# The last mixer's weights split early and kept in DRAM, with four side steps a chunk in its heads

## The reference, cut to what matters

```
x = first_block(x, ...)        # layer 0: short_conv_mixer, layer_norm, conv_ffn, layer_norm
                               # layer 1: diff_attention,   layer_norm, conv_ffn, layer_norm
return second_block(x, ...)    # h += ab_layer(rmsnorm(h)); h += cd_layer(rmsnorm(h)); rmsnorm(h)

def cd_layer(h, w_in, ..., w_glu, b_glu, lower_bound, hgrn_norm_g, w_out):      # the last mixer
    z = h @ w_in
    u, qd, fd, idd, gate = jnp.split(z, CD_SPLIT, axis=-1)
    yc = s5_mixer(u, ...)                      # y = scan over 256 steps; y * sigmoid(y @ w_glu + b_glu)
    f = lower_bound + (1.0 - lower_bound) * jax.nn.sigmoid(fd)
    od = chunked_gated_linear_attention(silu(qd), 1.0 - f, idd, log(f))         # 8 HGRN heads
    y = jnp.concatenate([yc, head_rmsnorm(od, hgrn_norm_g)], -1) * silu(gate)
    return y @ w_out
```

## Time and profile before

| | |
|---|---|
| median of three runs | 3274.36 us |
| profiled execution, its own time | 3276.79 us |
| its span, first to last instruction | 3275.4 us, mean granted TensorE clock 0.974 |
| TensorE matmul busy | 3078.6 us, 94% |
| VectorE busy | 2151.1 us, 66% |
| ScalarE busy | 1526.5 us, 47% |
| DMA | 596.74 MB, mean 182 GB/s |

### The profile page before, as it was taken

The page is one execution under the profiler, slowest core; times in us unless marked ns, Lnnn a source line. Parts: engine busy times, 40 slices in busy tenths (PEclk is TensorE's granted clock), DMA queues, the critical chain, the costliest instruction groups (busy, mean ns, idle before and its releaser), DMA issues. The chain is left out here.

```text
span 3275.4 us, 57220 instructions
## 1 busy us (share of the span) xinstructions
PE 3078.6 (94%) x25870; PEld 2610.3 (80%) x25870; DVE 2151.1 (66%) x2189; ACT 1526.5 (47%) x1393; POOL 65.8 (2%) x112
## 2 busy tenths in 40 slices
PE   8999899999999899998999999997999999788786
PEld 7888688888888787577888888886686787657685
DVE  5555666666555666457687786455665547998785
ACT  4343454545433444745455555334454534424543
POOL 0000000000000000001200000000000001000000
PEclk9999899999999999998999999999999999899898
DMA  8665355555665455453766666652445445554331
GB/s 282 206 206 201 108 206 206 199 200 198 214 206 194 142 176 171 154 168 126 265 227 216 221 225 231 207 193 94 166 155 184 164 168 186 173 196 145 120 121 65
DMA packets 295475, 596.74 MB, mean 182 GB/s; under 512 B 11824, under 2 KB 16048, under 8 KB 295104
## 3 DMA queue, kind: packets, MB, share of 16 engines
q1 hardware_dynamic: 287616, 564.22, 50.4%
q0 software_dynamic: 7616, 28.87, 2.4%
HBM read 577.32 MB, written 15.73 MB: 181 GB/s over the span
## 5 line engine op out<-in xcount | busy, mean ns | idle before, releaser
L1415 DVE TENSOR_TENSOR WL<-WF,WH 128x2048 bf16<-128x2048 f32 x533 | 1206.7, 2285 | 718.9 <-ACT WH L935 718.6
L504 PE MATMUL PSG<-XH,WH 128*128 128x256 bf16 x5648 | 1553.1, 275 | 53.9 <-DVE XL L1484 28.9
L504 PE MATMUL PSG<-XL,WH 128*128 128x256 bf16 x5648 | 1552.7, 275 | 0.0
L504 PE MATMUL PSG<-XH,WL 128*128 128x256 bf16 x5648 | 1552.1, 275 | 0.0
L935 ACT ACTIVATE WH<-WF 128x2048 bf16<-128x2048 f32 x533 | 1000.7, 1899 | 648.8 <-PE PSG L504 416.6
L504 PE MATMUL PSG<-SCR,WH 128*128 128x256 bf16 x4480 | 746.2, 275 | 0.0
L504 PEld LDWEIGHTS PSG<-XH,WH 128*128 128x128 bf16 x5648 | 557.2, 99 | 137.1 <-issue 65.6
L504 PE MATMUL PSG<-SCR,WL 128*128 128x256 bf16 x2240 | 614.8, 274 | 0.0
L504 PEld LDWEIGHTS PSG<-XL,WH 128*128 128x128 bf16 x5648 | 556.9, 99 | 70.5 <-issue 0.6
L504 PEld LDWEIGHTS PSG<-XH,WL 128*128 128x128 bf16 x5648 | 557.2, 99 | 69.2
L504 PEld LDWEIGHTS PSG<-SCR,WH 128*128 128x128 bf16 x4480 | 442.1, 99 | 58.8 <-issue 1.4
(11 more groups left out here) (232 smaller groups left out, 1569.4 us busy)
## 6 DMA issues: line engine op xcount, KB each, us to landing
WF<-ffn_w_up SPq DMA_DIRECT2D x176, 1024.0 KB, 5.8
WF<-ffn_w_down SPq DMA_DIRECT2D x88, 1024.0 KB, 5.1
WF<-ab_w_in SPq DMA_DIRECT2D x56, 1024.0 KB, 5.1
WF<-a_w_in SPq DMA_DIRECT2D x48, 1024.0 KB, 6.4
WF<-cd_w_in SPq DMA_DIRECT2D x48, 1024.0 KB, 5.2
WF<-a_w_out SPq DMA_DIRECT2D x16, 1024.0 KB, 5.2
WF<-kv_w_k SPq DMA_DIRECT2D x16, 1024.0 KB, 5.1
WF<-b_w_q SPq DMA_DIRECT2D x16, 1024.0 KB, 5.1
```

The costliest lines, as they stand in the source:

```text
L504: return nc.tensor.matmul(o, lhsT, rhs, start=start, stop=stop, skip_group_check=True)
L1415: tt(l, w, h, ALU.subtract).then_inc(s_lo, 1)
```

## The change

The kernel makes a plan of positions (`ring_plan`). All 533 chunks are multiplied as before. The 68 chunks of the last mixer are marked "kept": each is also given an earlier position of kind "keep", at which it is loaded in float32, split by ScalarE and VectorE into the next slot of the ring, and not multiplied; SyncE stores the slot's two halves (1 MB) to a DRAM tensor. The keep positions stand behind every fourth chunk of the first mixer's input weights from the ninth on, of up0 and of down0, behind every eighth of up1 and every third of down1. High and low halves now lie side by side in one buffer WS, so that one DMA moves both. At a chunk's own position in the last mixer SyncE loads the halves from DRAM into the slot, once the chunk or the store five positions before is done; ScalarE and VectorE do nothing for it, and TensorE waits on that DMA (d_ws). LA counts ring positions now, keep positions included.

The second change is in the last mixer's rates: four steps a chunk and not three for the second and third gate, glu, the fourth gate and cd_out0, on all three engines.

```
+def ring_plan(groups, stage, count):
+    def span(name):
+        a, b = stage[name][0], stage[name][-1]
+        return groups[a]["first"], groups[b]["first"] + len(groups[b]["rows"])
+    first_kept = span("u")[0]
+    after = set(range(8, span("mix")[1], 4))
+    for name, step in (("up0", 4), ("down0", 4), ("up1", 8), ("down1", 3)):
+        a, b = span(name)
+        after |= set(range(a + 1, b - 1, step))
+    after = sorted(after)[:count - first_kept]
+    plan = []
+    for i in range(count):
+        plan.append(("kept" if i >= first_kept else "mul", i))
+        if i in after:
+            plan.append(("keep", after.index(i)))
+    return plan, first_kept
...
-        WH = sb("WH", [128, RB, 4, 512], BF16)
-        WL = sb("WL", [128, RB, 4, 512], BF16)
+        WS = sb("WS", [128, RB, 2, 4, 512], BF16)
+        WH, WL = WS[:, :, 0, :, :], WS[:, :, 1, :, :]
...
+        def released(p):
+            kind, n = plan[p]
+            return (d_kept[n % 2], 16 * (n // 2 + 1)) if kind == "keep" else (s_mm, n + 1)
+        def split_done(p):
+            if plan[p][0] == "kept":
+                return d_ws[p % RB], 16 * len([q for q in range(p % RB, p + 1, RB) if plan[q][0] == "kept"])
+            return s_lo, raw_number[p] + 1
...
-            def load(i):
-                g, k0, rows = chunks[i]
+            def load(p):
+                if plan[p][0] == "kept":
+                    k = plan[p][1] - first_kept
+                    nc.sync.wait_ge(d_kept[k % 2], 16 * (k // 2 + 1))
+                    nc.sync.wait_ge(*released(p - RB))
+                    nc.sync.dma_start(WS[:, p % RB].rearrange("p h t n -> p (h t n)"), KEPT[k]).then_inc(
+                        d_ws[p % RB], 16)
+                    return
+                i = raw_number[p]
+                g, k0, rows = chunk_at(p)
...
                 if i >= RF:
                     nc.sync.wait_ge(s_lo, i - RF + 1)
                 nc.sync.dma_start(shaped(WF, i % RF, rows, g["width"]), src).then_inc(d_w[i % RF], 16)
+                if i >= RF and plan[raw[i - RF]][0] == "keep":
+                    q = raw[i - RF]
+                    k = plan[q][1]
+                    nc.sync.dma_start(KEPT[k], WS[:, q % RB].rearrange("p h t n -> p (h t n)")).then_inc(
+                        d_kept[k % 2], 16)
...
-                    nc.tensor.wait_ge(s_lo, i + 1)
+                    nc.tensor.wait_ge(*split_done(place[i]))
...
-            for gi in stage["cd_gate"][0:3]:
-                gemm(gi, xh, xl, rate=3)
+            for n, gi in enumerate(stage["cd_gate"][0:3]):
+                gemm(gi, xh, xl, rate=4 if n else 3)
...
-            residual("cd_out0", None, uh, ul, [(s_gl, 5 + k // 4) for k in range(8)], rate=3,
+            residual("cd_out0", None, uh, ul, [(s_gl, 5 + k // 4) for k in range(8)], rate=4,
...
-                if i >= RB:
-                    nc.scalar.wait_ge(s_mm, i - RB + 1)
-                act(shaped(WH, i % RB, rows, g["width"]), shaped(WF, i % RF, rows, g["width"]),
+                if p >= RB:
+                    nc.scalar.wait_ge(*released(p - RB))
+                act(shaped(WH, p % RB, rows, g["width"]), shaped(WF, i % RF, rows, g["width"]),
...
-            def hi_to(i):
-                while state["hi"] <= min(i, len(chunks) - 1):
+            def hi_to(p):
+                while state["hi"] < len(raw) and raw[state["hi"]] <= p:
...
-                    hi_to(g["first"] + c + LA)
+                    hi_to(place[g["first"] + c] + LA)
```

More of the change, by code:

```diff
@@ L227, in two_block_model @@
         d_w = [sem(f"d_w{i}") for i in range(RF)]
+        d_kept = [sem(f"d_kept{i}") for i in range(2)]
+        d_ws = [sem(f"d_ws{i}") for i in range(RB)]
         d_out = [sem(f"d_out{i}") for i in range(2)]
@@ L266, in two_block_model, with chunk_at @@
         groups, stage, chunks = weight_groups(A)
+        plan, first_kept = ring_plan(groups, stage, len(chunks))
+        KEPT = nc.dram_tensor("kept_weights", (len(chunks) - first_kept, 128, 2 * 2048), BF16).ap()
+        place = {n: p for p, (kind, n) in enumerate(plan) if kind != "keep"}
+        raw = [p for p, (kind, _) in enumerate(plan) if kind != "kept"]
+        raw_number = {p: n for n, p in enumerate(raw)}
+        def chunk_at(p):
+            kind, n = plan[p]
+            return chunks[n + first_kept if kind == "keep" else n]
+        def released(p):
+            kind, n = plan[p]
+            return (d_kept[n % 2], 16 * (n // 2 + 1)) if kind == "keep" else (s_mm, n + 1)
[3 more added lines that the diff above has]
+            return s_lo, raw_number[p] + 1
         def evac(gi):
@@ L422, in sync_program @@
             nc.sync.dma_start(POSI, A["positions"].partition_broadcast(128)).then_inc(d_pos, 16)
-            for i in range(RF, len(chunks)):
-                load(i)
+            for p in range(RF, len(plan)):
+                load(p)
             for g in range(4):
@@ L1372, in scalar_program @@
             for j, gi in zip(GATE_ORDER[0:3], gates[0:3]):
[L1373 removed]
+                keep(gi, four(GT1, j), 4 if j != 2 else 3, func=ACT.Silu)
             side.until(s5_flow)
             for j, gi in enumerate(stage["glu"]):
[L1376 removed]
+                ps = gemm(gi, rate=4)
                 nc.scalar.wait_ge(s_mm, done(gi))
@@ L1389, in scalar_program @@
             gated_0 = side.add_first(gated_s5(0))
-            keep(gates[3], four(GT1, 1), 3, func=ACT.Silu)
+            keep(gates[3], four(GT1, 1), 4, func=ACT.Silu)
             gated_1 = side.add_first(gated_s5(1))
@@ L1397, in scalar_program @@
             gated_h = side.add(gated_hgrn())
-            residual("cd_out0", None, rate=3, before=lambda c: side.until(gated_0, *((gated_1,) if c else ())))
+            residual("cd_out0", None, rate=4, before=lambda c: side.until(gated_0, *((gated_1,) if c else ())))
             side.until(gated_h)
@@ L1411, in lo, with lo_to @@
             def lo(i):
-                g, _, rows = chunks[i]
-                w, h, l = (shaped(t, i % n, rows, g["width"]) for t, n in ((WF, RF), (WH, RB), (WL, RB)))
+                p = raw[i]
+                g, _, rows = chunk_at(p)
+                w = shaped(WF, i % RF, rows, g["width"])
+                h, l = (shaped(t, p % RB, rows, g["width"]) for t in (WH, WL))
                 nc.vector.wait_ge(s_hi, i + 1)
                 tt(l, w, h, ALU.subtract).then_inc(s_lo, 1)
-            def lo_to(i):
-                while state["lo"] <= min(i, len(chunks) - 1):
+            def lo_to(p):
+                while state["lo"] < len(raw) and raw[state["lo"]] <= p:
                     lo(state["lo"])
@@ L1424, in gemm @@
                 for c in range(len(g["rows"])):
-                    lo_to(g["first"] + c + LA)
+                    lo_to(place[g["first"] + c] + LA)
                     if before:
@@ L2054, in vector_program @@
             gates = stage["cd_gate"]
-            for gi in gates[0:3]:
-                gemm(gi, rate=3)
+            for n, gi in enumerate(gates[0:3]):
+                gemm(gi, rate=4 if n else 3)
             side.until(s5_flow)
             for j, gi in enumerate(stage["glu"]):
-                gemm(gi, rate=3)
+                gemm(gi, rate=4)
                 for n in range(0, 4, 2):
@@ L2073, in vector_program @@
             gated_0 = side.add_first(gated_s5(0))
-            gemm(gates[3], rate=3)
+            gemm(gates[3], rate=4)
             gated_1 = side.add_first(gated_s5(1))
```

10 lines of the change are left out of this document (6 added, 4 removed).

## The result

The changed kernel takes 3285.1 us, the median of seven runs (3279.1 to 3296.0), against 3274.4 before: ratio 1.0032, 95% interval 1.0020 to 1.0044. The forecast was 3238, in a range of 3198 to 3274. Rival C, the slower one, named the direction and the place; its price was 117 us of costs, and the stages ahead of the last mixer cost 87 in the profiled execution.

A forecast was written before the change was run, and what follows sets the result against it. VectorE, with the serial head chains, was taken to bound the last mixer and TensorE the rest. Gains of 72 less costs of 36 took 36 off 3276.8, giving 3241, or 3238 us as median; range 3198 to 3274.

The forecast's parts named there:

- Rival C: Ring of three f32 buffers: loads land 2 us or more later, up groups stall; costs 117, total 3319 us; chance 0.12.
- Gain 1: Last mixer, fd/qd/idd, 24 chunks: without splits VectorE is no longer late, TensorE idle and clock loss shrink; 28 us.
- Gain 2: Last mixer, gates to cd_out1: four side steps a chunk and no splits on VectorE; 44 us.
- bound from above: Upper limit set for Gain 2, with 3 us of waits and no clock loss: 55 us.
- The bare stretch: Between cd_out0 and cd_out1: 12 leftover HGRN steps run without chunks, 19.6 us; its 11.4 us of idle time would go.
- Rival B: Serial chains, not VectorE's load, hold the last mixer: gains only 36, total 3274 us; chance 0.13.
- rival D: Kept chunks' loads come late to the last mixer; only a landing four times today's would matter; chance 0.01.
- cost 1: Up stages: kept chunks shorten look-ahead at group ends, and up0's fifth split is late; 14 us, up1 4.
- cost 3: DMA: added stores and loads bring only down1 to the edge, 337 of 340 GB/s; 3 us, 2 for other stages.
- Cost 2: Start of up0 and up1: the split TensorE wants as third chunk after the layer norm is 2.5 us late; 5 together.
- At nothing: The 68 early splits, store issue, kept loads and slot reuse cost nothing, as VectorE has slack under TensorE.
- the signs named beforehand: Right: ffn_w_up landing at or below 6.5 us, down1 233 to 240; wrong: up0 over 500, down1 over 250, last mixer over 520.

The follow-up runs named there:

- e3: Kernel before with only the new side-step rates (four a chunk from the second gate on), splits where they were: 3275.8 us, ratio 1.0002.
- e4: Changed kernel with the old rates, three side steps a chunk throughout: 3283.7 us, ratio 1.0030.
- e5: Changed kernel with the look-ahead counted in TensorE chunks, so a kept chunk takes none of its three: 3282.5 us, ratio 1.0015.
- e9: e5 with the early load of each kept chunk cut to 256 of 1024 KB, splits and stores whole: 3242.4 us, ratio 0.9899.
- e13: e9 with the S5 rotation-table pieces every fourth chunk of up1 instead of every fifth: 3220.1 us, ratio 0.9835.
- e17: Changed kernel with kept chunks moved to cheap places, rates of three, look-ahead in chunks, table pieces every fourth chunk and eight chunks later: 3215.1 us, ratio 0.9812.
- e18: Kernel before with only the rotation-table pieces moved: every fourth chunk and started eight chunks later: 3269.6 us, ratio 0.9979.
- e2: Changed kernel with stores cut to 256 of 4096 columns, every kept load reading the first slot: 3271.3 us, ratio 0.9993.
- e6: Changed kernel keeping every fourth chunk in down1 instead of every third, three kept chunks going to v: 3274.9 us, ratio 0.9995.
- e10: Changed kernel with no chunk kept in up0 and up1 but spread over other stages, rates of three, look-ahead in chunks: 3250.5 us, ratio 0.9927.
- e16: Kernel before with only the rotation-table pieces moved to every fourth chunk of up1: 3281.8 us, ratio 1.0023.
- e11: As e10, but eleven kept chunks in up0, one after every eighth chunk, instead of in the first mixer's ab_out, va, ka, qa: 3227.7 us, ratio 0.9855.
- e1: Changed kernel with keep positions in up0 and up1 one chunk later in the group: 3388.5 us, ratio 1.0354.

## Why the forecast was wrong

**Gain 1** was right: 28 forecast, 30.6 measured, TensorE's side idle 8.2 us for 7.

**Gain 2** came near in its sum and was wrong in its reason, so the nearness is luck. 44 were forecast and 38.6 came. (Its bound from above is added wrongly: with 3 us of waits and no clock loss its own terms give 146.7 + 64 - 16 + 3 = 198 of 258, a gain of 63 with the 2 behind it, and not 55. Nothing hangs on it.) The bare stretch went, as said, but e3 and e4 show that removing it is worth nothing: the same steps then lengthen the gates. With the old rates the gain is 45.2. The term that I gave to the bare stretch belonged to VectorE's splits. Rival B, chains that hold the last mixer at a gain of 36, falls, and rival D with it: the kept halves land after 4.8 us, and TensorE never waits for them in the last mixer.

**The steps that failed are cost 1, in up1 above all, and cost 3.** Costs of 36 were forecast and 87 came: up1 took 18.6 more than its 16.5, down1 17.8 more than its 3, up0 9.0 more than its 14.5, the rest 5.6. Of cost 1, in up0 the mechanism is the one in the text, the fifth split behind a load issued at the second split's end. Its size was too small and the place was only half seen. The text has the fifth split end 12.3 us after the first split ended; the trace has 515.04 less 501.8 (499.57 and one split), 13.2, because that load took 6.8 us and not 5.9. So 1.1 us a pair became 1.2 to 2.0 at the g group's third chunk, 16.0 us over ten pairs where 12 were written. I also took the stall for one of look-ahead, which e5 refutes: what binds is the ring's period. In up1 the term was 14 and the stalls made 30.5, beside 4.6 at the stage's start. Three of them make 20.5: 2.6 and 8.7 at the 25th and 27th chunk, 9.2 at the 67th. The text took from up1's extra 8.6 us that the table flow made VectorE late "at some ends", and took two full ones. That was a misreading: in the kernel before all of up1's chunks behind the first are 5.2 us long but the 25th, 12.3, and just ahead of it ScalarE waits 11.6 us for the rotation store. So one stall makes 7.0 of the 8.6 us, and it is not one of look-ahead. With kept chunks the pieces began to cost as well, where one falls on a group's end (the 27th and 67th chunk here; those at the 47th and 87th cost nothing in this kernel, and did in e9). e13 takes the pieces' stalls away, e17 and e18 that of the store.

**Cost 2**: 2.5 a stage was forecast, from the time at which the split ends; the third chunk was 6.0 and 5.8 us late. TensorE waits 2.9 us and the next 5.2 us have a granted clock of 0.50, the 1.2 GHz level, so the wait counts twice. That row stands above. e5, without the wait, has in the same window:

```profile
391.60:396.80 5.20, 5.20 (x51) 4.66 (x49) 4.96 (x10) 2.74 (x2) 0.00 (x0) 1.00 0.75 242
```

That is 51 matmuls instead of 25.

**Cost 3**, 3 us in down1, was 20.8. Mean demand against mean capacity (337 of 340 GB/s) was the wrong question. With landings of 9.3 us for stores and 9.7 for the kept chunks' loads (above), ScalarE waits 117.6 us for loads in down1. Before, it waited 101.2 us there for TensorE and 11.3 for loads, so it had time to spare:

```profile
ACT WS L993 <- DMA WF<-ffn_w_down: 61.2, 35, 5.3
ACT WS L993 <- DMA WF<-cd_w_out: 56.4, 14, 4.7
```

Without the stored bytes (e2) or with one kept chunk in four (e6) the loss is 4, and the kept chunks' loads land after 5.9 and 7.5 us. The stage moved 307 GB/s at a share of 0.88, so a mean capacity of 349, but its rate in 40 equal slices runs up and down:

```profile
GB/s 349 303 175 237 370 402 250 348 391 196 373 336 204 405 247 363 388 158 373 350 219 396 223 260 389 230 365 377 157 384 325 223 402 217 318 331 239 363 290 361
```

The Trainium skill (DMA: Bandwidth & Descriptors, Specifications) has about 358 GB/s for a core's HBM limit. The trace doesn't hold a slice to it (405 at most), with one core at work; and neither limit would have told of the 21 us. The prediction's capacity of 340 GB/s is passed by slices too, so it was a mean and no limit.

**At nothing** held where it was about VectorE's busy time: e9 has every split and no loss in up0. It would not have held everywhere: in e10 a kept chunk costs 1.3 us in kq to b_out and 1.5 in the ab mixer.

**Rival C** was right in its lever: its own point was an added landing of about 1 us, and the fifth load, at 6.8, had 0.9. It was given a chance of 0.12. It wrote all groups off at 2 us; the trace has about 1.5 us in every second one. Of the signs named beforehand, both of being wrong that concern the early stages came (up0 500.5, down1 253.5), while the median landing of the ffn_w_up loads, 6.2 us, stayed under the 6.5 that was to show the forecast right. The median of a stage says nothing of the one load that the group waits for.

Open is what the first mixer gains (-3.6 in after, -3.9 in e16, which has no kept chunk), which is likely the spread of single executions; and why kq's first groups pay most (+5.2 and +4.5 us at its first and fifth chunk in e11).

## What to carry to other kernels

Extra work under a bound engine has to fit at the place where it is put, not only into the mean slack of the stage. The test is the ring's period, the time in which one buffer is loaded, split and free again: here one more load in every four chunks went through three float32 buffers and cost 1.5 us per two groups, one in eight cost nothing, with VectorE over a quarter idle in both. Ask for each added split when its load is issued and how long it lands there, keep stores out of the burst of loads, and look for other flows that fall on the same chunk as yours every so often. A bare stretch of leftover steps is not a cost by itself: fill it only if the stretch that takes the steps has room for them.

## What the hardware showed that was not expected

A 1 MB store from SBUF took 8.9 us to land at the median and 10.2 in e9's up0, where a 1 MB load into the split ring took 4.8. A load issued 4 us behind such a store took 10.4 us at the median (e1), against 6.4 for one issued 10 to 12 us behind it. A wait of 2.9 us was followed by 5.2 us at the 0.50 clock, in which 25 matmuls ran instead of 51: the small stall near a stage's start cost its length again. A faster filler can slow a kernel: moving the table pieces earlier lengthened the wait for one store from 11.6 to 19.1 us.
